# Earlier first loads of a mixture of experts, and another last norm, in a hybrid decoder step on one core

## What is computed

```python
# h = rmsnorm(x) * norm_ffn_g
logits = h @ router_w + router_b                 # 32 experts
top_logit, top_e = lax.top_k(logits, 4)
gate = jax.nn.softmax(top_logit, axis=-1)
# for each expert e, on the tokens that chose it:
hg, hu = jnp.split(xblk @ w_gu[e] + b_gu[e], 2, axis=-1)
hg = jnp.minimum(hg, 7.0); hu = jnp.clip(hu, -7.0, 7.0)
act = (hu + 1.0) * hg * jax.nn.sigmoid(1.702 * hg)
y = act @ w_down[e] + b_down[e]
# x = x + sum of gate * y over the four experts; the output is rmsnorm(x) * norm_final_g
```

## Time and profile before

| what | us |
|---|---|
| median of 3 runs | 1516.85 (1515.31 to 1519.12) |
| the profiled execution | 1517.89 |
| its span in the trace | 1515.5 |
| PE busy | 1404.4 (93%) |
| VectorE busy | 459.5 (30%) |
| ScalarE busy | 241.1 (16%) |
| DMA | 471.74 MB, mean 311 GB/s |

### The profile page before, as it was taken

The page is one execution under the profiler, slowest core; times in us unless marked ns, Lnnn a source line. Parts: engine busy times, 40 slices in busy tenths (PEclk is TensorE's granted clock), DMA queues, the critical chain, the costliest instruction groups (busy, mean ns, idle before and its releaser), DMA issues.

```text
span 1515.5 us, 21428 instructions
## 1 busy us (share of the span) xinstructions
PE 1404.4 (93%) x8699; PEld 714.2 (47%) x8699; DVE 459.5 (30%) x880; ACT 241.1 (16%) x455; POOL 106.8 (7%) x174
## 2 busy tenths in 40 slices
PE   6987799999999979999999999999999999999996
PEld 4755568866666644343343343343333433433433
DVE  5788664533312231121121121121122112211213
ACT  3211332110414021011011011010010110110111
POOL 1189700000000000000000000000000000000000
PEclk9998889997999989999999999999999999999997
DMA  7943111011667729999999999999999999999991
GB/s 313 180 121 62 56 63 58 30 57 29 267 264 300 339 81 420 389 428 426 428 428 428 429 428 428 429 428 429 428 428 428 428 428 429 428 428 429 428 390 43
DMA packets 42736, 471.74 MB, mean 311 GB/s; under 512 B 4913, under 2 KB 10161, under 8 KB 11185
## 3 DMA queue, kind: packets, MB, share of 16 engines
q1 hardware_dynamic: 36672, 461.42, 72.9%
q10 hardware_dynamic: 6000, 9.41, 3.4%
HBM read 465.07 MB, written 5.74 MB: 311 GB/s over the span
## 4 chain that ended last, share of the span: by engine, by line
PE 66%; DMA 24%; DVE 5%; issue 4%; ACT 1%; SPq 0%; ACTq 0%; DVEq 0%
DMA big<-in_w_gu 23%; PE bank L1136 15%; PE bank L1089 13%; PE bank L638 10%; PE bank L1027 6%; PE bank L721 2%; PE bank L891 2%; PE bank L815 1%; PE bank L1157 1%; PE bank L1035 1%; PE bank L1111 1%; PE bank L807 1%; PE bank L782 1%; PE bank L790 1%; PE bank L872 1%
## 5 line engine op out<-in xcount | busy, mean ns | idle before, releaser
L1089 PE MATMUL bank<-big 128*64 128x512 f32 x2048 | 455.6, 603 | 36.8 <-DMA big<-in_w_gu 36.1
L1089 PEld LDWEIGHTS bank<-big 128*64 128x64 f32 x2048 | 153.6, 139 | 331.6 <-issue 310.6
L1136 PE MATMUL bank<-big 128*64 128x512 f32 x1024 | 223.4, 594 | 0.0
L638 PE MATMUL bank<-big 128*128 128x320 f32 (+1 forms) x688 | 188.6, 431 | 2.2 <-ACT big L1343 1.3
L1964 DVE TENSOR_TENSOR big<-big,bank 128x320 f32<-128x320 f32 x128 | 62.4, 487 | 337.7 <-PE bank L1157 332.3
L638 PEld LDWEIGHTS bank<-big 128*128 128x128 f32 x688 | 130.8, 192 | 57.6 <-issue 7.2
L1952 DVE TENSOR_SCALAR big<-bank 128x512 f32<-128x512 f32 x32 | 22.2, 693 | 389.5 <-PE bank L1089 389.4
L1136 PEld LDWEIGHTS bank<-big 128*64 128x64 f32 x1024 | 74.5, 137 | 136.8 <-issue 134.9
L1196 ACT ACTIVATE big<-bank 128x320 f32<-128x320 f32 (+3 forms) x122 | 53.1, 435 | 278.1 <-PE bank L638 57.1
L1413 ACT ACTIVATE big<-big 128x512 f32<-128x512 f32 x32 | 20.1, 628 | 483.2 <-DVE big L1952 483.2
L1027 PE MATMUL bank<-big 128*128 128x512 f32 x204 | 92.4, 602 | 0.8 <-DVE big L1907 0.8
(11 more groups left out here) (368 smaller groups left out, 1183.3 us busy)
## 6 DMA issues: line engine op xcount, KB each, us to landing
big<-in_w_gu SPq DMA_DIRECT2D x128, 2048.0 KB, 25.4
big<-in_w_down SPq DMA_DIRECT2D x64, 2048.0 KB, 24.0
big<-in_dense SPq DMA_DIRECT2D x47, 1024.0 KB, 8.2
big<-u_windows ACTq DMA_DIRECT2D x32, 160.0 KB, 7.4
out_y<-big SPq DMA_DIRECT2D x3, 512.0 KB, 2.6
big<-in_smw SPq DMA_DIRECT2D x1, 1408.0 KB, 19.6
big<-in_xT SPq DMA_DIRECT2D x2, 640.0 KB, 4.6
big<-in_consts SPq DMA_DIRECT2D x1, 1028.5 KB, 14.7
```

Of the source, the lines that this page charges most:

```text
L638: last = mm(b[:, 0:n], w[:, k, :], src[:, k, :], start=(k == 0), stop=(k == kt - 1))
L1089: last = mm(ps[n][part, :], xte[:, 2 * j + k, part], w[s][:, k, n * 512:n * 512 + 512], start=False, stop=end)
L1136: last = mm(ps[bank][part, :], actT[:, 4 * d + i, part], w[s][:, i, h * 512:h * 512 + 512], start=(d == 0 and i == 0), stop=end)
```

## The change

Six edits:

1. `rbias` is loaded some loads earlier in SyncE's queue, ahead of the fifth load of the weights.
2. The mask is made by one comparison and two additions in place of three comparisons and a reduction; `sel` is made straight from the positions, ahead of the rest of the table.
3. The first gather is done in halves: half 0 before `start_bias`, half 1 and its transposes between the quarters j = 0 and j = 1 and in the middle of j = 1 of the first up projection. The counts move behind the transposes of half 0.
4. `start_bias` goes from the end of a pair to the beginning of the next, so the last pair has none after it and line 1173 goes.
5. The down biases are laid out over four groups of 32 rows, and four of them are issued together ahead of four sums.
6. `most_tokens` is read before the loop, and the four tests stand inside one test. The final gain becomes a diagonal matrix `gdiag`, so that matmuls make rows and gain together, in six banks; the square root takes scale and epsilon with it, its table is loaded ahead, and the last products are shared by VectorE and ScalarE.

```diff
+            most = most_tokens(eng)
             with eng.Fori(1 if first else 0, NP // 2) as e:
                 two(e, e)
-            most = most_tokens(eng)
-            with eng.Fori(1, PASSES) as p:
-                with eng.If(most > p * CAP):
+            with eng.If(most > CAP):
+                with eng.Fori(1, PASSES) as p:
+                    with eng.If(most > p * CAP):
...
+                    sp.dma_start(rbias, bass.AP(a["router_b"].tensor, 0, [[0, P], [1, NE]])).then_inc(S("rbias_in"), 16)
...
-            sp.dma_start(rbias, bass.AP(a["router_b"].tensor, 0, [[0, P], [1, NE]])).then_inc(S("rbias_in"), 16)
...
-            def gather():
+            def gather(h):
                 for t in range(TT):
-                    for h in range(2):
-                        last = mm(ps[5 + h][:, :], sel[:, t, :], htok[:, t, h * 512:h * 512 + 512], start=(t == 0), stop=(t == TT - 1))
+                    last = mm(ps[5 + h][:, :], sel[:, t, :], htok[:, t, h * 512:h * 512 + 512], start=(t == 0), stop=(t == TT - 1))
...
+                if first:
+                    for bank in (4, 5, 6):
+                        pe.wait_ge(psum_free[bank], BANK_USES[bank])
+                    pe.wait_ge(S("selected"), 1)
+                    stored(pe, "th20")
+                    gather(0)
...
+                start_bias()
+                if first:
+                    pe.wait_ge(psum_free[5], ahead(5, "gather"))
+                    gathered(0)
+                    counts()
+                    pe.wait_ge(psum_free[4], ahead(4, "rows"))
                 for j in range(4):
...
+                    if first and j == 1:
+                        stored(pe, "th21")
+                        gather(1)
+                    if first and j == 2:
+                        pe.wait_ge(psum_free[6], ahead(6, "rows"))
...
+                        if first and (j, k, n) == (1, 1, 0):
+                            pe.wait_ge(psum_free[6], ahead(6, "gather"))
+                            gathered(1)
...
-                start_bias()
...
-                    if n == 3:
+                    if n == (0 if first else 3):
                         pe.wait_ge(psum_free[4], nth(4, "down", it))
-                    if n >= 4:
+                    if first and n % 4 == 0:
+                        for i in range(n, n + 4):
+                            if n:
+                                pe.wait_ge(psum_free[SUM_BANK[i]], nth(SUM_BANK[i], f"sum{i - 4}", it))
+                            down_bias(i, ps[SUM_BANK[i]])
+                    elif n >= 4:
...
-                        last = nc.tensor.transpose(ps[2 + 2 * t + h][0:tile_rows[t], i * P:(i + 1) * P],
-                                                   xT[:, 4 * h + i, t * P:t * P + tile_rows[t]], ident)
+                    last = mm(ps[Y_BANK[2 * t + h]][0:tile_rows[t], i * P:(i + 1) * P], xT[:, 4 * h + i, t * P:t * P + tile_rows[t]],
+                              gdiag[:, 4 * h + i, :], start=True, stop=True)
...
-            for n in (2, 3):
-                mm(ps[n][:, :], biasrow[32 * n:32 * n + 32, :], bias[32 * n:32 * n + 32, :], start=False, stop=True)
...
             last.then_inc(S("y_sum"), 1)
+            y_tokens(1, 0)
...
             last.then_inc(S("y_sum_tok"), 1)
-            pe.wait_ge(S("y_var"), 1)
-            y_tokens(2)
+            for t, h in ((1, 1), (2, 0), (2, 1)):
+                y_tokens(t, h)
...
+            step(af(view(EPS + 2, 1), view(EPS, 1), ACT.Sqrt))
...
+            for t in range(TT):
+                act.wait_ge(S("y_tok"), 2 * t + 2)
+                rows = slice(0, tile_rows[t])
+                step(af(yout[rows, t, 512:D], ps[Y_BANK[2 * t + 1]][rows, :], ACT.Identity, scale=rxt[rows, t:t + 1]), "final_act")
...
+            step(tt(eq4, over(over(con("iota")[:, 0:NE], 1, TOPK), 1, TT), over(idxf[:, :, 0:TOPK], 3, NE), ALU.is_equal))
+            step(tt(eqg[:, :, 0:2], eq4[:, :, 0:2], eq4[:, :, 2:4], add))
+            step(tt(mask, eqg[:, :, 0], eqg[:, :, 1], add))
...
-            step(v.reduce_sum(mask, eq4.rearrange("p t r e -> p t e r"), AX.X))
...
+            step(stt(ranks.rearrange("p (t s) -> p t s", s=2), b[:, :, 0:2], 1.0, mask[:, :, 0:2], add, mul))
+            step(stt(sel6, iota, 1.0, over(ranks, 2, CAP), add, ALU.is_equal), "selected")
...
-                for h in range(2):
-                    part = slice(h * 512, h * 512 + 512)
-                    step(stt(yout[rows, t, part], ps[2 + 2 * t + h][rows, :], rxt[rows, t:t + 1], gfin[rows, part], mul, mul), "final")
+                step(ts(yout[rows, t, 0:512], ps[Y_BANK[2 * t]][rows, :], rxt[rows, t:t + 1], None, mul), "final_dve")
```

More of the change, by code:

```diff
@@ L583, in _ @@
             load_pair(1, 1, 1)
+            most = most_tokens(sp)
             with sp.Fori(1, NP // 2) as e:
                 load_two(e, e)
[L586 to L590, removed]
+            with sp.If(most > CAP):
+                with sp.Fori(1, PASSES) as p:
+                    with sp.If(most > p * CAP):
+                        with sp.Fori(0, NP // 2) as e:
+                            load_two(p * (NP // 2) + e, e)
             for t in range(TT):
-                sp.wait_ge(S("final"), 2 * t + 2)
-                sp.dma_start(o["y"][:, t], yout[:, t]).then_inc(S("y_out"), 16)
+                rows = slice(0, tile_rows[t])
+                sp.wait_ge(S("final_dve"), t + 1)
+                sp.wait_ge(S("final_act"), t + 1)
+                sp.dma_start(o["y"][rows, t], yout[rows, t]).then_inc(S("y_out"), 16)
             sp.wait_ge(S("stores"), 16 * 3)
@@ L1014, in _ @@
             end_job(mm(b[:, 2 * NE:TT * NE], ones, mask[:, 1], start=False, stop=True), "pos")
[L1015 to L1018, removed]
             sides = [(0, slice(0, CAP)), (1, slice(CAP, 2 * CAP))]
[L1023 removed]
+            def gather(h):
                 for t in range(TT):
[L1026 to L1029 removed]
+                    last = mm(ps[5 + h][:, :], sel[:, t, :], htok[:, t, h * 512:h * 512 + 512], start=(t == 0), stop=(t == TT - 1))
+                last.then_inc(psum_full[5 + h], 1)
             def gathered(h):
@@ L1042, in start_bias, with counts @@
                     mm(ps[n][:, :], biasrow[row, :], bias[row, :], start=True, stop=False)
[L1044 to L1052, removed]
-            start_bias()
[L1054 to L1060, removed]
+            def counts():
+                b = start_job("cnt")
+                for s in range(TT):
+                    last = mm(b[:, 0:NE], ones, mask[:, s, :], start=(s == 0), stop=(s == TT - 1))
+                end_job(last, "cnt")
             def gates_across():
@@ L1070, in down_bias @@
             def down_bias(n, b):
-                row = slice(32 * (n // 2), 32 * (n // 2) + 32)
-                mm(b[:, 0:T], bdown[row, n % 2, :], gateT[row, :], start=True, stop=False)
+                row = slice(32 * (n % 4), 32 * (n % 4) + 32)
+                mm(b[:, 0:T], bdown[row, n // 4, :], gateT[row, :], start=True, stop=False)
             def loaded(n, r, odd):
@@ L1104, in expert @@
                 pe.wait_ge(S("selected"), it + 2)
-                gather()
+                gather(0)
+                gather(1)
                 columns = hact.rearrange("p (h c i) -> p h i c", h=2, i=4)
@@ L1140, in expert @@
                         last.then_inc(S("load_used"), 1)
[L1141 to L1144, removed]
                 if first:
@@ L1436, in _ @@
                 step(af(ysqT[:, k, :], xT[:, k, :], ACT.Square), "y_sq")
-            act.wait_ge(S("y_var"), 1)
-            step(af(rxt, rxt, ACT.Sqrt), "y_sqrt")
+            act.wait_ge(S("y_sum_tok"), 1)
+            step(af(rxt[:, 0:2], ps[7][:, 0:2], ACT.Sqrt, scale=1.0 / D, bias=eps_rms), "y_sqrt")
+            step(af(rxt[0:CAP, 2:3], ps[7][0:CAP, 2:3], ACT.Sqrt, scale=1.0 / D, bias=eps_rms[0:CAP]), "y_sqrt")
+            act.wait_ge(S("y_factor"), 1)
+            for t in range(TT):
+                act.wait_ge(S("y_tok"), 2 * t + 2)
+                rows = slice(0, tile_rows[t])
+                step(af(yout[rows, t, 512:D], ps[Y_BANK[2 * t + 1]][rows, :], ACT.Identity, scale=rxt[rows, t:t + 1]), "final_act")
         @block.gpsimd
@@ L1911, in _ @@
             step(tt(g4, g4, over(gsum, 2, TOPK), mul))
-            for t in range(TT):
-                step(tt(eqg[:, t], eq4[:, t], over(g4[:, t], 2, NE), mul))
+            step(tt(eqg, eq4, over(g4, 3, NE), mul))
             step(v.reduce_sum(gate, eqg.rearrange("p t r e -> p t e r"), AX.X))
@@ L1924, in _ @@
             step(cp(most_i32[:, :], gsum[:, 0:1]), "counts")
+            dve.wait_ge(S("gfin_in"), 16)
+            step(tt(gdiag, gdiag, over(con("ident"), 1, KT), mul), "gain")
             def next_pass(p):
```

53 lines of the change are left out of this document (24 added, 29 removed).

## The result

The changed kernel takes 1504.82 us in the median of 5 executions (1501.18 to 1506.56), the one before 1516.85 (1515.27 to 1519.12): a ratio of 0.990, 95% interval 0.9875 to 0.9934. So it is faster, by 12.0 us where 17.9 were forecast (the forecast was 1499.0, its range 1495.5 to 1505.0).

The account below looks back on a forecast made before the run. Bound by the router and first gather until 567 us, then DMA's weight stream, then PE alone at the end. Savings 6.6 + 1.1 + 3.4 + 6.6 + 0.2 = 17.9 us from 1516.85 gave 1499.0, range 1495.5 to 1505.0.

Parts of the forecast that it names:

- what sets the stream: Weight loads: the issue after the second pair's first quarter, the last place the stream waits for PE, sets all that follows.
- the terms of the front: Work up to the second pair's first quarter: 2.1 + 4.5, so the stream restarts for good 6.6 us earlier.
- the read: ScalarE's read of `most_tokens` ahead of the first pair's sigmoid: 1.3 us, of which 1.2 reaches PE.
- the down biases: First pair, from the down projection's end to the next up projection: 8.1 us in place of 12.6, saved 4.5.
- the tests: VectorE's read and four tests before `experts_done`: one test with one jump, 0.9 us in place of 4.30, saved 3.4.
- rival (d): Pairs lengthened by the moved `start_bias`, PE sets the period; gain gone at 5.2 us per pair, 1520 at 5.5; chance 0.02.
- now PE is idle for 1.5 us, so I take full clock: Ahead of `y_tokens`: PE's idle time is short, so eight records are priced at 0.14 us each, not 0.23.
- rival (a): PE's clock is at half at the end, some 3.8 us more, time 1503; chance 0.17.
- PE starts at 0.35: Start of `y_tokens`: PE begins 0.35 us after `experts_done`, as line 1173 and the wait for PE are gone.
- Rival (c): The single far jump costs an instruction fetch, 2.5 us in place of 0.9, time 1500.6; counted within the forecast's 0.60.
- token rows: From `experts_done` to the end of the last product: 10.0 us in place of 16.6, saved 6.6.
- the stores: End of the kernel: 0.2 us saved on the last store, which has half the rows.

Follow-up runs that it names:

- u1_rbias_late: The changed kernel with the router's bias loaded late again, all else kept; median 1505.79 us.
- c1_combined: The changed kernel with spare matmuls in the router and ahead of the last quarters, and ScalarE's read of `most_tokens` ahead of its copy of the gates; median 1497.49 us.
- n1_no_further_passes: The changed kernel without the code for the further passes, so no jump over them; median 1500.48 us.
- u3_down_bias_one_by_one: The changed kernel with the first pair's down biases again one ahead of each sum, in two groups of rows; median 1508.38 us.
- w1_spare_matmuls: The changed kernel with three spare matmuls of 448 columns ahead of the last quarter of each up projection in the loop; median 1499.30 us.

## Why the prediction was right in its way and 6 us off in its size

**Right: what sets the stream.** The step that all hung on was that the second pair's issue, and not the first restart, sets everything behind it. In thirteen profiles the distance from that issue to the last quarter is 827.0 to 827.8 us, while the issue itself moved by 10.3 us. The undone halves are the sharpest test: the first restart moved by 3.5 us, the second issue by 0.3.

**Right in sum, partly by luck: the terms of the front.** Forecast 6.6, measured 6.76. Counted from the eighth load, the bias gave 3.05 (3.0), mask and selection 1.46 (1.4), and the part from the gather to the up projection 2.97 (2.0), so the up projection starts 7.5 us earlier and not 6.4. The first up projection with the second half inside it is 3.75 us longer (3.1), the read costs 0.8 (1.2), and from the down projection's end to the next up projection it is 12.59 less 8.74, which is 3.85 (4.5). The errors cancelled: the up projection's start and the read came out 1.5 us better than forecast, the second half and the down biases 1.3 us worse.

**Right: the tests, by a lucky pick.** Forecast 0.9 from the last addition to `experts_done`, measured 0.86; but the prediction chose it between 0.4 and 2.5 without a row. `start_bias` 1.07, measured 1.06.

**Lucky: that the median is inside the range.** It lies 0.2 us below the upper bound of 1505.0, and two of the five executions lie above it. In rival (d) eleven pairs with 3.3 us of slack give 4.9 us as the point at which the gain is gone, and not 5.2; this changes nothing.

**Wrong: "now PE is idle for 1.5 us, so I take full clock".** PE was idle for 2.41 us up to 1488.11, and the clock fell in this execution; by the prediction's own words, half clock in the `y_tokens` is a sign that it is wrong. The price is in rival (a), which I gave 0.17. But it is not a rival that comes true or not: the same code had full clock in u1_rbias_late (idle 2.17 us) and c1_combined (2.47), and low clock after 2.15 to 2.44 us in six others. It should have been a share of the executions, in the sum.

**Wrong: "PE starts at 0.35", and no gap.** PE started at 1.02, since its jump was not over, and stood still for 1.10 more in the midst of the records. Rival (c) had this mechanism but priced it on VectorE alone, where it was small. Together: token rows forecast 10.0, measured 13.5. Against n1_no_further_passes (8.94) the start costs 0.7, the gap 1.1 and the clock 2.8 (16, 16 and 8 records in 3.11, 2.29 and 1.70 us, where they took 2.02, 1.22 and 1.09); the rest of the forecast was 1.1 too high. With full clock and no gap, c1_combined (9.72) and n1_no_further_passes reach the forecast.

**Not seen at all: the last quarter's clock.** In the chain of the kernel before five of twelve last quarters took 8.56 to 8.79 us and seven 7.09, the last of them among these. I took that one as it stood in one execution. In the middle these don't count, since DMA sets the pace; the last one costs 1.69 in full.

**Wrong in sign, small: the stores.** Forecast 0.2 less, measured 0.58 more. They are issued within 2.6 us now, where before the products spaced them out over 3.5, and from 1500 to 1502 us the DMA engines move over 400 GB/s. That the last store waits for the two before it is the likely reason; no run tests it.

## What to carry to other kernels

When a stream of loads stops and restarts several times, find the last stop that PE causes: only work ahead of that one moves the end, and it may lie a whole stage behind the stop that the bandwidth row shows first. A jump over code that is not run should be priced on each engine for itself (here 0.6 us on VectorE, and 2.1 to 2.6 us from PE's last record to its next), before that engine's work is planned to the tenth of a microsecond. Where PE idles for some microseconds ahead of work on the path, the clock belongs into the sum as a share of executions, and spare matmuls in the idle time are a cheap test, if the engine really is idle there and not busy with a branch.

## What the runs showed of the hardware that was not expected

- PE's granted clock fell to its lower level after idle times of 2.1 to 2.7 us in some cases and not in others of the same length. Of the last quarters in the changed kernel's chain, each after such a wait, six of twelve were at 8.8 us and six at 7.1, mostly two or three of a kind in a row. Ahead of the token rows, with 2.1 to 2.5 us idle, it fell in six profiles and stayed in three. With the wait filled by matmuls none of the fourteen last quarters was slow in w1_spare_matmuls, and none of the fourteen in c1_combined.
- Behind the far jump PE delivered twelve records and then stood still for 0.27 to 1.63 us in five profiles (with matmuls and with transposes), thirteen and 0.56 us in a sixth, three and 2.39 us in a seventh, and had no gap in three. Without the jump there was none in the one profile taken.
- Four float32 matmuls on four groups of 32 rows take 0.82 us together, where in u3_down_bias_one_by_one each takes 0.73 us between two sums.
